# Opening, two attention starts and GpSimd's pieces rearranged in a two-layer transformer kernel

## The chip, the core and the metric

The kernel runs on one core of a Trainium2 chip. TensorE (PE) does the matrix products, VectorE (DVE), ScalarE (ACT) and GpSimd (POOL) the rest, and SyncE (SP) issues most of the DMA transfers. The metric is the device time of one execution in microseconds; less is better.

## What is computed

Two transformer layers in succession on 512 tokens of width 1024, in float32. The first has 16 meta tokens ahead of the sequence, and begins like this:

```python
xn = rms_norm(h, norm1_g)
p = xn @ w_in
(u_pool, q, c_lat, q_idx, k_idx, w_idx, cb, cc, cu, g_raw) = split_columns(p)
c_lat = rms_norm(c_lat, kv_norm_g)
attn = dsa_attention(q, q_idx, w_idx, c_lat, k_idx)   # scores by index heads choose 128 keys
h = h + (sigmoid gates over pooled, attention and convolution branches) @ w_o
h = h + (silu(gate) * up) @ w_down
```

The second layer has a feed-forward part, a mixer with two attentions (forgetting attention on 8 heads, stick-breaking attention on 8 heads), a second feed-forward part and a gated embedding.

## The kernel before

Everything lies transposed, features on the 128 partitions and tokens along the free dimension. The work is cut into 173 chunks of weights. A chunk has eight k-steps of 128 rows and 256 columns of weights (2048 columns per partition), and makes two output tiles, t = 0 and t = 1.

Each float32 operand is split into a high part (rounded to the matmul's type) and a low part (the rest), and each product is made of three matmuls: high by high, high by low, low by high (`passes`, L677 to L679). For the weights of a chunk this is a pipeline over four engines: SP loads `raw`, ScalarE copies the high part to `whi` (`high`, L1150, counted by `w_hi`), GpSimd subtracts to get the low part `wlo` (`low`, L561, in four pieces, counted by `w_lo`), and TensorE runs the chunk. There are two buffers, by the parity of the chunk: ScalarE begins with a chunk's high part when TensorE has ended the chunk two before. The input is split the same way, row by row of 128 features: `xh` on ScalarE (`gained`, L1155), `xl` on VectorE (`split`, L1602).

The order of the work on each engine is written out by hand, and semaphores join the engines; there is no planner.

The opening: chunk 0 (C_LAT) holds the latents. Its second tile is made by `index_tile`, which needs the index weights in a stacked tile, `stk`: the high part in columns 0 to 39, the low part in 64 to 103. ScalarE writes the high part behind the eighth row, GpSimd the low part (L580, `stk_lo`). Chunk 1 (C_QI) holds the index queries, chunks 2 to 5 (C_Q and on) the queries. Within chunk 1 come the norm sums (`norm_sums`, L746), for which VectorE adds up squares in `ssum`; then ScalarE takes a square root and VectorE a reciprocal (L1631), and the latents are scaled with it. VectorE splits `qst`, the stacked index queries, at L1767, and the scores of the index heads run between the k-steps of chunk 3 and on.

The first attention runs between the k-steps of four chunks, C_GB to C_GB + 3, by a list of slots:

```python
DSA_STEPS = {6 + n * 54 // (QB * HEADS + QB - 1): n for n in range(QB * HEADS + QB)}
```

In step n TensorE makes the logits of unit n + 2, transposes the probabilities of unit n and multiplies earlier ones with the values. VectorE copies a 16 x 16 corner out of PSUM (`dsa_edge`, L1934) and into its place (`dsa_edge_in`, L1943); TensorE waits for both.

The second layer's attentions run between the k-steps of chunks C_SQ and on, and before them stand eight head norms (`head_root` on ScalarE, `head_normed` on VectorE) and the values of chunk C_FV1 (`values_high` on ScalarE, `values_low` on VectorE, which frees the PSUM tile).

Of the kernel before, what the change touches and what calls it, by code (L numbers as in the profile page):

```python
# [82 lines left out]
DSA_STEPS = {6 + n * 54 // (QB * HEADS + QB - 1): n for n in range(QB * HEADS + QB)}  # L83

# [35 lines left out]
def build(nc, I, out):  # L120
    with ExitStack() as ctx:
# [265 lines left out]
        def _(sp):  # L387
# [46 lines left out]
            sp.dma_start(raw[:, 0, DK * P:DK * (P + KW)], I["w_lat"][:, DK * P:DK * (P + KW)]).then_inc(kw_in, 16)  # L434
# [106 lines left out]
        def _(pool):  # L541
# [37 lines left out]
            pool.wait_ge(stk_hi, 1)  # L579
            pool.tensor_tensor(stk[:, :, 64:64 + KW], raw[:, 0, DK * P:DK * (P + KW)].rearrange("p (k n) -> p k n", k=DK),  # L580
                               stk[:, :, 0:KW].bitcast(F32), ALU.subtract).then_inc(stk_lo, 1)
# [3 lines left out]
            run(C_Q, C_D[0], 2)  # L585
# [88 lines left out]
        def _(pe):  # L674
# [10 lines left out]
            def index_tile(b):  # L685

                pe.wait_ge(stk_lo, 1)
                for k in range(DK):
                    for z in range(2):
                        cs = slice(HALF * z, HALF * z + HALF)  # L690
                        if k:
                            pe.matmul(ps[0:KW, b + z, 0:HALF], stk[:, k - 1, 0:KW], xl[:, k - 1, cs], start=False, stop=False)
                        if k == DK - 1:
                            pe.matmul(ps[0:KW, b + z, 0:HALF], stk[:, k, 0:KW], xl[:, k, cs], start=False, stop=False)
                        mm = pe.matmul(ps[:, b + z, 0:HALF], stk[:, k, :], xh[:, k, cs], start=k == 0, stop=k == DK - 1)
                mm.then_inc(tile_done, 1)

            def chunk(c, hi, lo, per=0, i=None, X=None, full=(False, False), widths=(P, P), between=None, steps=None, ready=None):


                s, w = c % 2, sum(widths) if c != C_LAT else P
                if c not in (C_LAT, C_QI):
                    pe.wait_ge(w_lo, lin(c + 1, per, i))
                for t in range(2):
                    if C_GB < c < C_WB or C_SQ <= c < C_MX:
                        pe.wait_ge(acc_free, 2 * (c - 1) + t + 1)
                    elif c >= 2:
                        pe.wait_ge(acc_free, lin(2 * (c - 2) + t + 1, 2 * per, i))
                    b, m, o0 = bank(c, t), widths[t], sum(widths[:t])
                    if c == C_LAT and t == 1:  # L710
                        index_tile(b)
                        continue
                    for k in range(DK):
                        if X is not None:
                            x_ready(X, k, t)
                        if c in (C_LAT, C_QI) and t == 0 and k % 2 == 0:
                            if k < 6:
                                pe.wait_ge(lat_lo if c == C_LAT else qi_part_lo, k // 2 + 1)
# [85 lines left out]
            chunk(C_LAT, xh, xl, X=0, full=(True, True), widths=(P, KW))  # L804
            chunk(C_QI, xh, xl, steps=lambda t, k: norm_sums(0, C_QI) if (t, k) == (0, 5) else None)
# [333 lines left out]
        def _(act):  # L1139

            act.dma_start(vec[:, 0:V_ROWS], I["vec"]).then_inc(vec_in, 16)
            act.preload_act_table_set("sqrt_and_others")
# [33 lines left out]
            def root(S):  # L1176
                act.wait_ge(ss_done, S + 1)
                if S == 0:
                    act.activation(rt[:, 0:HALF], ps[:, 5, 0:HALF], ACT.Sqrt, bias=eps[:], scale=1.0 / D)
                    act.activation(rt[:, HALF:TM], ps[:, 7, 0:HALF], ACT.Sqrt, bias=eps[:], scale=1.0 / D).then_inc(rt_done, 1)  # L1180
# [45 lines left out]
            for n in range(DK):  # L1226
# [5 lines left out]
                if n == 0:  # L1232
# [3 lines left out]
            act.wait_ge(kw_in, 16)  # L1236
            act.wait_ge(stk_zero, 1)
            act.activation(stk[:, :, 0:KW], raw[:, 0, DK * P:DK * (P + KW)].rearrange("p (k n) -> p k n", k=DK),
                           ACT.Copy).then_inc(stk_hi, 1)
# [11 lines left out]
            high(C_LAT + 2)  # L1251
            act.wait_ge(ones_done, 1)
# [17 lines left out]
            act.activation(rt[:, 0:HALF], ps[:, 5, 0:HALF], ACT.Sqrt, bias=eps[:], scale=1.0 / D_LAT)  # L1270
            act.activation(rt[:, HALF:TM], ps[:, 7, 0:HALF], ACT.Sqrt, bias=eps[:], scale=1.0 / D_LAT).then_inc(crt_done, 1)
# [53 lines left out]
            with act.Fori(0, 2) as i:  # L1325
                for q in range(2):
# [5 lines left out]
                    high(c + 4, 6, i)  # L1332
# [26 lines left out]

            query_high(1)  # L1360
# [7 lines left out]
            dsa_unit(0)  # L1368
            dsa_unit(1)
            for slot in range(4 * 2 * DK):  # L1370
                n = DSA_STEPS.get(slot)
                if n is not None:
# [6 lines left out]
                    if n % QB == 1 and (n + 7) // QB < HEADS:  # L1379
                        query_high((n + 7) // QB)  # L1380
                    if n + 2 < QB * HEADS:
                        dsa_unit(n + 2)
                if slot % (2 * DK) == 2 * DK - 1:
                    high(C_GB + slot // (2 * DK) + 2)
# [100 lines left out]
            stack_high(F, 1, qF, kF, qt1, kt1)  # L1485
            head_root(6)
            head_root(7)
            for t in range(2):
                values_high(C_FV1, t, vF, 0)
# [102 lines left out]
        def _(dve):  # L1592
# [35 lines left out]
            def root(S):  # L1628
                lo = 0 if S == 0 else META
                dve.wait_ge(rt_done, S + 1)  # L1630
                dve.reciprocal(rs[:, lo:TM], rt[:, lo:TM]).then_inc(rs_done, 1)  # L1631
# [94 lines left out]
            dve.memset(eps[:], EPS)  # L1726
            dve.memset(stk[:].bitcast(F32), 0.0).then_inc(stk_zero, 1)
            dve.memset(ones[:].bitcast(F32), 1.0).then_inc(ones_done, 1)
# [5 lines left out]
            for n in range(DK):  # L1734
                split(0, n, V_N1, lo=0)
            dve.wait_ge(w_lo, C_LAT + 1)
# [12 lines left out]
            root(0)  # L1749
# [72 lines left out]
            dve.wait_ge(crt_done, 1)  # L1822
            link(dve.reciprocal(rc[:], rt[:]))
# [125 lines left out]

            for j in range(1, QB + 1):  # L1950
                link(dve.memset(pT[:, j, seen_from(j):P * j], 0.0))
            for n in range(2):
                dsa_unit(n)
                normalise(A, n, pr[:, n % 2, 0:META + P * (n % QB + 1)])
            query_low(1)
            for slot in range(4 * 2 * DK):
# [7 lines left out]
                if n % QB == QB - 1 and n >= QB:  # L1964
# [106 lines left out]
            head_normed(5)  # L2071
            head_normed(6)
            head_normed(7)
            for t in range(2):
                values_low(C_FV1, t, vF, 0, t + 3)
# [147 lines left out]
```

## Time and profile before

| | |
|---|---|
| median of 3 runs | 2006.44 us (2006.27 to 2006.93) |
| the profiled execution | 2006.25 us, span 2004.4 us |
| PE busy | 1989.6 us, 99% |
| POOL busy | 1007.8 us, 50% |
| DVE busy | 887.9 us, 44% |
| ACT busy | 730.2 us, 36% |
| the chain that ended last | 96% PE |

The span runs from the first to the last instruction of the profile, and the execution's time lies 1.85 us above it. PE's busy time counts the modelled ends of pipelined matmuls, so the distance from one start to the next tells more than the length of one. The column in brackets of a timeline is the idle time of the engine ahead of an instruction, and whose work ended it.

### The profile page before, as it was taken

To read this page: it belongs to the slowest core of one execution; us is meant where nothing else is said; L and a number is where in the kernel's file an instruction comes from. 1 tells how busy PE (TensorE), PEld (TensorE's weight loads), DVE (VectorE), ACT (ScalarE), POOL (GpSimd) and SP (SyncE) were. 2 spreads that over 40 slices of the span, in tenths; PEclk is the share of its full clock that TensorE was granted. 3 is DMA by queue.
4 is the path that set the end of the run, shared out by engine and by line. 5 is a ranking of instruction groups with operands and counts; after the bars stand their busy time and mean duration, and the time that the engine had idled before them with its cause. 6 is when DMAs were issued, how large, how long until landed. Compare 5 with 4: busy or idle time off the path is not lost.

```text
span 2004.4 us, 26695 instructions
## 1 busy us (share of the span) xinstructions
PE 1989.6 (99%) x9495; PEld 1667.9 (83%) x9495; DVE 887.9 (44%) x1468; ACT 730.2 (36%) x1017; POOL 1007.8 (50%) x780
## 2 busy tenths in 40 slices
PE   8999999999999999999999999999999999999999
PEld 7898887788888888888888888889888888888887
DVE  6687756634433222153333214677645533332124
ACT  6413224434323223232222225667643422222232
POOL 5344542245555554455555446665555555555443
PEclk9999999999999999999999999999999999999999
DMA  5223232123333322333332332332222333332232
GB/s 175 90 85 104 86 105 64 43 76 92 105 92 96 105 92 82 100 104 98 90 105 79 100 111 89 93 101 81 82 87 84 105 102 86 105 90 93 96 109 85
DMA packets 253787, 188.81 MB, mean 94 GB/s; under 512 B 6609, under 2 KB 249681, under 8 KB 253681
## 3 DMA queue, kind: packets, MB, share of 16 engines
q1 hardware_dynamic: 253024, 187.53, 31.4%
q8 instruction: 44, 0.72, 0.2%
q10 hardware_dynamic: 688, 0.31, 0.1%
q14 instruction: 31, 0.25, 0.0%
HBM read 180.93 MB, written 2.10 MB: 91 GB/s over the span
## 4 chain that ended last, share of the span: by engine, by line
PE 96%; DVE 1%; ACT 1%; issue 1%; DMA 0%; SPq 0%; DVEq 0%; ACTq 0%
PE ps L677 30%; PE ps L678 30%; PE ps L679 29%; PE ps L933 1%; PE ps L1085 1%; PE ps L1005 1%; PE ps L1006 1%; PE ps L1007 1%; PE ps L1073 1%; PE ps L1072 0%; PE ps L927 0%; DMA raw<-in_w_in 0%; DVE ssum L1748 0%; PE ps L1055 0%; PE ps L826 0%
## 5 line engine op out<-in xcount | busy, mean ns | idle before, releaser
L561 POOL TENSOR_TENSOR wlo<-raw,whi 128x512 fp32r<-128x512 f32 (+1 forms) x624 | 856.9, 1405 | 867.7 <-ACT whi L1150 850.3
L677 PE MATMUL ps<-xh,whi 128*128 128x512 f32 (+1 forms) x1888 | 722.2, 383 | 7.2 <-DVE xl L1602 5.8
L679 PE MATMUL ps<-xh,wlo 128*128 128x512 f32 (+1 forms) x1888 | 714.5, 378 | 0.0
L678 PE MATMUL ps<-xl,whi 128*128 128x512 f32 (+1 forms) x1888 | 714.4, 378 | 0.0
L1150 ACT ACTIVATE whi<-raw 128x2048 fp32r<-128x2048 f32 x154 | 289.6, 1881 | 775.1 <-PE ps L679 775.0
L677 PEld LDWEIGHTS ps<-xh,whi 128*128 128x128 f32 x1888 | 355.8, 188 | 72.2 <-DVE xl L1602 5.8
L679 PEld LDWEIGHTS ps<-xh,wlo 128*128 128x128 f32 x1888 | 355.6, 188 | 66.5
L678 PEld LDWEIGHTS ps<-xl,whi 128*128 128x128 f32 x1888 | 356.3, 189 | 61.8 <-issue 0.7
L1662 DVE TENSOR_TENSOR tmp<-ps,rs 128x512 f32<-128x512 f32 x148 | 101.9, 691 | 314.5 <-PE ps L679 297.0
L677 PE MATMUL ps<-fh,whi 128*128 128x512 f32 x528 | 205.4, 389 | 0.0
L678 PE MATMUL ps<-fl,whi 128*128 128x512 f32 x528 | 205.4, 389 | 0.0
L679 PE MATMUL ps<-fh,wlo 128*128 128x512 f32 x528 | 205.4, 389 | 0.0
L1602 DVE SCALAR_TENSOR_TENSOR hT<-ps,hT 128x512 f32 x40 | 27.6, 690 | 270.8 <-PE ps L679 269.9
L1687 DVE TENSOR_TENSOR tmp<-tmp 128x512 f32<-128x512 f32 x66 | 90.3, 1369 | 111.8 <-ACT tmp L1192 111.6
L679 PEld LDWEIGHTS ps<-fh,wlo 128*128 128x128 f32 x528 | 99.1, 188 | 20.7
L677 PEld LDWEIGHTS ps<-fh,whi 128*128 128x128 f32 x528 | 99.1, 188 | 20.5
L678 PEld LDWEIGHTS ps<-fl,whi 128*128 128x128 f32 x528 | 99.1, 188 | 20.5
L628 POOL TENSOR_TENSOR wlo<-raw,whi 128x384 fp32r<-128x384 f32 (+1 forms) x84 | 75.7, 933 | 38.2 <-ACT whi L1497 37.1
L1155 ACT ACTIVATE xh<-hT,vec (+1 forms) x48 | 34.7, 727 | 127.2 <-DVE hT L1602 125.2
L1194 ACT ACTIVATE fh<-tmp 128x512 f32 x66 | 41.8, 633 | 101.4 <-DVE tmp L1687 101.4
L1690 DVE TENSOR_TENSOR fl<-tmp,fh 128x512 f32 x66 | 50.9, 772 | 61.2 <-ACT fh L1194 61.2
L1602 DVE SCALAR_TENSOR_TENSOR xl<-hT,vec,xh (+1 forms) x48 | 45.6, 955 | 57.9 <-ACT xh L1155 57.9
(324 smaller groups left out, 2215.3 us busy)
## 6 DMA issues: line engine op xcount, KB each, us to landing
raw<-in_w_in SPq DMA_DIRECT2D x87, 512.0 KB, 4.6
raw<-in_w_gate_up SPq DMA_DIRECT2D x44, 512.0 KB, 4.6
raw<-in_ffn_w_gate SPq DMA_DIRECT2D x44, 512.0 KB, 4.0
raw<-in_ffn_w_up SPq DMA_DIRECT2D x44, 512.0 KB, 5.2
raw<-in_ffn_w_down SPq DMA_DIRECT2D x32, 512.0 KB, 4.1
raw<-in_w_down SPq DMA_DIRECT2D x16, 512.0 KB, 4.0
raw<-in_ffn_w_down SPq DMA_DIRECT2D x16, 384.0 KB, 3.7
raw<-in_w_b SPq DMA_DIRECT2D x8, 512.0 KB, 4.0
```

Of the source, the lines that this page charges most:

```text
L561: ins = pool.tensor_tensor(wlo[:, c % 2, cs], raw[:, c % 2, cs], whi[:, c % 2, cs].bitcast(F32), ALU.subtract)
L628: ins = pool.tensor_tensor(wlo[:, c % 2, cs], raw[:, c % 2, cs], whi[:, c % 2, cs].bitcast(F32), ALU.subtract)
L677: pe.matmul(o, w_of(whi), xhi, start=first, stop=False)
L678: pe.matmul(o, w_of(whi), xlo, start=False, stop=False)
L679: return pe.matmul(o, w_of(wlo), xhi, start=False, stop=last)
L1150: act.activation(whi[:, c % 2, 0:n], raw[:, c % 2, 0:n], ACT.Copy).then_inc(w_hi, 1)
L1155: act.activation(one(xh, nn)[:, lo:TM], one(hT, nn)[:, lo:TM], ACT.Copy, scale=col(vec, lin(gain + n, per, i))).then_inc(xh_done, 1)
L1194: act.activation(one(fh, lin(n, per, i)), tmp[:, 3, :], ACT.Copy).then_inc(h_hi, 1)
L1602: return dve.scalar_tensor_tensor(o, a, s, b, op0, op1)
L1662: dve.tensor_tensor(o, ps[0:o.shape[0], bank(c, t), :], rsx[0:o.shape[0]], ALU.mult).then_inc(acc_free, 1)
L1687: dve.tensor_tensor(tmp[:, 3, :], tmp[:, 1, :], tmp[:, 2, :], ALU.mult).then_inc(h_done, 1)
L1690: dve.tensor_tensor(one(fl, nn), tmp[:, 3, :], one(fh, nn).bitcast(F32), ALU.subtract).then_inc(h_split, 1)
```

## The change

- Opening: ten matmuls on `ones` run first on TensorE, into a bank not yet in use. The latents and the index weights' tile, one after the other before, are now interleaved by rows: three rows of latents, then the wait for `stk_lo`, then rows of both in turn. The index weights are loaded, copied (ScalarE) and reduced (now on VectorE) behind the third row instead of behind the eighth.
- Chunk 2's weights go through ScalarE and GpSimd in four quarters, for which TensorE waits one by one, as chunk 1's did. The norm sums move from (t, k) = (0, 5) to (1, 2).
- The root of the first norm and that of the latents' norm become Ln and Exp on ScalarE, without VectorE's reciprocal.
- GpSimd's `low` works in eight pieces instead of four, in every chunk that goes through it.
- First attention: ScalarE's weight copies of three chunks go as quarters into slots without a step; its last weight copy before the attention is taken out of the loop, which is unrolled. On VectorE the first two units stand ahead of the clearing of `pT`, and `dsa_edge(n)` ahead of `dsa_edge_in(n - 1)`.
- Second layer: the copies of the first value tile of C_FV1 move ahead of the last two head roots and norms.

```diff
+FREE_SLOTS = [slot for slot in range(4 * 2 * DK) if slot not in DSA_STEPS]
...
                 sp.dma_start(hT[:, n, :], I["h0"][P * n:P * n + P, :]).then_inc(x_in[n], 16)
-            sp.dma_start(raw[:, 0, DK * P:DK * (P + KW)], I["w_lat"][:, DK * P:DK * (P + KW)]).then_inc(kw_in, 16)
+                if n == 2:
+                    sp.dma_start(raw[:, 0, DK * P:DK * (P + KW)], I["w_lat"][:, DK * P:DK * (P + KW)]).then_inc(kw_in, 16)
...
             sp.wait_ge(stk_lo, 1)
+            sp.wait_ge(w_lo, C_LAT + 1)
...
             def low(c, per=0, i=None):
-                n = n_cols(c) // 4
+                n = n_cols(c) // 8
                 pool.wait_ge(w_hi, lin(c + 1, per, i))
-                for part in range(4):
+                for part in range(8):
...
+            for z in range(4):
+                if z < 3:
+                    pool.wait_ge(qi_part_hi, 4 + z)
+                else:
+                    pool.wait_ge(w_hi, C_Q + 1)
+                cs = slice(CH // 4 * z, CH // 4 * z + CH // 4)
+                pool.tensor_tensor(wlo[:, 0, cs], raw[:, 0, cs], whi[:, 0, cs].bitcast(F32),
+                                   ALU.subtract).then_inc(qi_part_lo if z < 3 else w_lo, 1)
...
+            def index_row(k):
...
+                    if k:
+                        pe.matmul(ps[0:KW, b + z, 0:HALF], stk[:, k - 1, 0:KW], xl[:, k - 1, cs], start=False, stop=False)
+                    if k == DK - 1:
+                        pe.matmul(ps[0:KW, b + z, 0:HALF], stk[:, k, 0:KW], xl[:, k, cs], start=False, stop=False)
+                    mm = pe.matmul(ps[:, b + z, 0:HALF], stk[:, k, :], xh[:, k, cs], start=k == 0, stop=k == DK - 1)
...
+            def opening():
+
+                pe.wait_ge(ones_done, 1)
+                for n in range(10):
+                    pe.matmul(ps[:, 7, :].rearrange("p (a t) -> p a t", a=4), ones[:],
+                              ones[:].unsqueeze(1).to_broadcast([P, 4, P]), start=True, stop=True)
+                for k in range(3):
+                    latent_row(k)
+                    latent_low(k)
                 pe.wait_ge(stk_lo, 1)
...
+                index_row(0)
+                index_row(1)
+                for k in range(3, DK):
+                    latent_row(k)
+                    index_row(k - 1)
+                    latent_low(k)
+                index_row(DK - 1)
...
+            opening()
+            chunk(C_QI, xh, xl, steps=lambda t, k: norm_sums(0, C_QI) if (t, k) == (1, 2) else None)
...
+                    act.activation(rt[:, 0:HALF], ps[:, 5, 0:HALF], ACT.Ln, bias=eps[:], scale=1.0 / D)
+                    act.activation(rt[:, HALF:TM], ps[:, 7, 0:HALF], ACT.Ln, bias=eps[:], scale=1.0 / D).then_inc(rt_done, 1)
+                    act.wait_ge(rt_done, 1)
+                    act.activation(rs[:], rt[:], ACT.Exp, scale=-0.5).then_inc(rs_done, 1)
...
+                if j and z < 4:
+                    high_quarter(C_GB + j + 1, z)
...
+                if n == 2:
+                    dve.wait_ge(stk_hi, 1)
+                    dve.tensor_tensor(stk[:, :, 64:64 + KW], raw[:, 0, DK * P:DK * (P + KW)].rearrange("p (k n) -> p k n", k=DK),
+                                      stk[:, :, 0:KW].bitcast(F32), ALU.subtract).then_inc(stk_lo, 1)
...
+                if n < QB * HEADS:
+                    dsa_edge(n)
                 if 1 <= n <= QB * HEADS:
                     dsa_edge_in(n - 1)
-                if n < QB * HEADS:
-                    dsa_edge(n)
...
+            values_low(C_FV1, 0, vF, 0, 3)
             head_normed(6)
             head_normed(7)
-            for t in range(2):
-                values_low(C_FV1, t, vF, 0, t + 3)
+            values_low(C_FV1, 1, vF, 0, 4)
```

`latent_row(k)` makes the high by high and low by high matmuls of the latents' row k (four of 264 columns), `latent_low(k)` the two with `xl`.

## Rows read from the trace of the kernel before

**Rows 1.** The page, busy time by engine.

```profile
PE 1989.6 (99%) x9495; PEld 1667.9 (83%) x9495; DVE 887.9 (44%) x1468; ACT 730.2 (36%) x1017; POOL 1007.8 (50%) x780
```

**Rows 2.** TensorE's waits: releaser, us in total, times, longest.

```profile
PE ps L677 <- DVE xl L1602: 5.8, 1, 5.8
PE ps L677 <- DVE vF L1602: 1.4, 1, 1.4
PE ps L933 <- DVE edge L1934: 1.4, 4, 0.7
PE ps L927 <- DVE edge L1934: 0.9, 2, 0.7
PE ps L746 <- DVE ssum L1748: 0.7, 1, 0.7
```

**Rows 3.** Timeline of TensorE, opening: start, length (us), line, operands, count.

```profile
11.37 0.28 PE L677 MATMUL ps<-xh,whi 128*128 128x264 f32 x1
...
18.17 0.39 PE L677 MATMUL ps<-xh,whi 128*128 128x512 f32 x1
...
23.13 1.16 PE L746 MATMUL ps<-ssum,ones 128*128 128x264 f32 x4 [0.69 <-DVE ssum L1748]
...
30.94 0.39 PE L677 MATMUL ps<-xh,whi 128*128 128x512 f32 x1
...
36.38 1.05 PE L812 MATMUL ps<-sq,ones 128*128 128x264 f32 x4
...
43.29 0.39 PE L677 MATMUL ps<-xh,whi 128*128 128x512 f32 x1
```

**Rows 4.** Timeline of GpSimd, opening and a feed-forward stage.

```profile
3.76 0.73 POOL L577 TENSOR_TENSOR wlo<-raw,whi 128x256 fp32r<-128x256 f32 x1 [0.51 <-ACT whi L1230]
...
33.90 7.01 POOL L561 TENSOR_TENSOR wlo<-raw,whi 128x512 fp32r<-128x512 f32 x4 [3.84 <-ACT whi L1150]
...
45.55 5.03 POOL L561 TENSOR_TENSOR wlo<-raw,whi 128x512 fp32r<-128x512 f32 x4 [4.63 <-ACT whi L1150]
...
559.66 5.94 POOL L561 TENSOR_TENSOR wlo<-raw,whi 128x512 fp32r<-128x512 f32 x4 [4.94 <-ACT whi L1150]
```

**Rows 5.** Timeline of ScalarE, opening.

```profile
7.00 1.41 ACT L1155 ACTIVATE xh<-hT,vec 128x528 fp32r<-128x528 f32 x2 [0.38 <-DMA hT<-in_h]
...
12.17 0.45 ACT L1238 ACTIVATE stk<-raw 128x320 fp32r<-128x320 f32 x1
...
31.93 1.90 ACT L1150 ACTIVATE whi<-raw 128x2048 fp32r<-128x2048 f32 x1
```

**Rows 6.** Timeline of VectorE, opening.

```profile
7.76 1.45 DVE L1602 SCALAR_TENSOR_TENSOR xl<-hT,vec,xh 128x528 fp32r<-128x528 f32 x2 [0.65 <-ACT xh L1155]
...
25.27 3.45 DVE L1631 RECIPROCAL rs<-rt 128x528 f32<-128x528 f32 x1 [2.20 <-ACT rt L1180]
...
35.34 7.90 DVE L1767 TENSOR_TENSOR qst<-qiT,qih 32x1024 fp32r<-32x1024 f32 x4 [1.20 <-ACT qih L1263]
```

**Rows 7.** Timeline of SyncE, opening: the index weights' transfer.

```profile
6.42 0.43 SPq L434 DMA_DIRECT2D raw<-in_w_lat  x1
```

**Rows 8.** VectorE's line L1767: ns min/median/max, first and last start.

```profile
L1767 DVE TENSOR_TENSOR qst<-qiT,qih x4: 1219/2192/2204, 35.3 to 42.0; 32x1024 fp32r<-32x1024 f32 x4
```

**Rows 9.** Timeline of VectorE, first attention.

```profile
359.33 1.21 DVE L1943 COPY pT<-edge 16x16 f32<-16x16 f32 x1
```

**Rows 10.** Timeline of GpSimd, first attention.

```profile
359.23 5.67 POOL L561 TENSOR_TENSOR wlo<-raw,whi 128x512 fp32r<-128x512 f32 x4 [20.74 <-ACT whi L1150]
```

**Rows 11.** Timeline of ScalarE, end of the first attention.

```profile
395.18 0.60 ACT L1349 ACTIVATE pT<-ps 128x512 f32<-128x512 f32 x1
...
404.63 1.92 ACT L1150 ACTIVATE whi<-raw 128x2048 fp32r<-128x2048 f32 x1 [1.64 <-PE ps L679]
```

**Rows 12.** Timeline of VectorE and ScalarE, before the second attention.

```profile
1276.69 3.38 DVE L1602 SCALAR_TENSOR_TENSOR kF<-qs,vec,rtq 128x512 f32<-128x512 f32 x2
...
1283.26 1.55 ACT L1433 ACTIVATE vF<-ps,rtok 128x256 fp32r<-128x256 f32 x4
```

More of the change, by code:

```diff
@@ L683, in x_ready @@
                     pe.wait_ge(x_split, DK * X + k + 1)
-            def index_tile(b):
-                pe.wait_ge(stk_lo, 1)
[L688 to L696, printed above, removed]
+            def index_row(k):
+                b = bank(C_LAT, 1)
+                for z in range(2):
+                    cs = slice(HALF * z, HALF * z + HALF)
+                    if k:
[3 more added lines that the diff above has]
+                    mm = pe.matmul(ps[:, b + z, 0:HALF], stk[:, k, :], xh[:, k, cs], start=k == 0, stop=k == DK - 1)
+                if k == DK - 1:
+                    mm.then_inc(tile_done, 1)
@@ new lines, in latent_row @@
+            def latent_row(k):
+                b, w = bank(C_LAT, 0), slice(P * k, P * k + P)
+                halves = [(ps[:, b + z, 0:HALF], slice(HALF * z, HALF * z + HALF)) for z in range(2)]
+                pe.wait_ge(xh_done, k + 1)
+                for o, cs in halves:
+                    pe.matmul(o, whi[:, 0, w], xh[:, k, cs], start=k == 0, stop=False)
+                if k % 2 == 0:
+                    if k < 6:
+                        pe.wait_ge(lat_lo, k // 2 + 1)
+                    else:
+                        pe.wait_ge(w_lo, C_LAT + 1)
+                for o, cs in halves:
+                    pe.matmul(o, wlo[:, 0, w], xh[:, k, cs], start=False, stop=False)
@@ new lines, in latent_low @@
+            def latent_low(k):
+                w = slice(P * k, P * k + P)
+                pe.wait_ge(x_split, k + 1)
+                for z in range(2):
+                    mm = pe.matmul(ps[:, bank(C_LAT, 0) + z, 0:HALF], whi[:, 0, w], xl[:, k, HALF * z:HALF * z + HALF],
+                                   start=False, stop=k == DK - 1)
+                if k == DK - 1:
+                    mm.then_inc(tile_done, 1)
+            def opening():
[6 more added lines that the diff above has]
+                    latent_low(k)
+                pe.wait_ge(stk_lo, 1)
+                index_row(0)
[5 more added lines that the diff above has]
+                index_row(DK - 1)
@@ L698, in chunk @@
             def chunk(c, hi, lo, per=0, i=None, X=None, full=(False, False), widths=(P, P), between=None, steps=None, ready=None):
-                s, w = c % 2, sum(widths) if c != C_LAT else P
-                if c not in (C_LAT, C_QI):
+                s, w = c % 2, sum(widths)
+                if c not in (C_QI, C_Q):
                     pe.wait_ge(w_lo, lin(c + 1, per, i))
@@ L715, in chunk @@
                             x_ready(X, k, t)
-                        if c in (C_LAT, C_QI) and t == 0 and k % 2 == 0:
+                        if c in (C_QI, C_Q) and t == 0 and k % 2 == 0:
                             if k < 6:
-                                pe.wait_ge(lat_lo if c == C_LAT else qi_part_lo, k // 2 + 1)
+                                pe.wait_ge(qi_part_lo, 3 * (c - C_QI) + k // 2 + 1)
                             else:
@@ L1250, in _ @@
                 act.activation((sq, rt)[n % 2][:], hT[:, n, :], ACT.Square).then_inc(sq_done, 1)
-            high(C_LAT + 2)
-            act.wait_ge(ones_done, 1)
+            for z in range(4):
+                if z == 0:
+                    act.wait_ge(raw_in[0], raw_level(C_Q, 0, None))
+                    act.wait_ge(tile_done, 2 * C_LAT + 2)
+                cs = slice(CH // 4 * z, CH // 4 * z + CH // 4)
+                act.activation(whi[:, 0, cs], raw[:, 0, cs], ACT.Copy).then_inc(qi_part_hi if z < 3 else w_hi, 1)
             root(0)
@@ L1324, in _ @@
             act.preload_act_table_set("sigmoid_and_others")
-            with act.Fori(0, 2) as i:
+            for i in range(2):
                 for q in range(2):
@@ L1368, in _ @@
             dsa_unit(0)
+            high_quarter(C_GB + 1, 0)
             dsa_unit(1)
+            high_quarter(C_GB + 1, 1)
             for slot in range(4 * 2 * DK):
                 n = DSA_STEPS.get(slot)
+                j = slot // (2 * DK)
+                z = FREE_SLOTS.index(slot) - len([f for f in FREE_SLOTS if f < 2 * DK * j]) if slot in FREE_SLOTS else 4
+                if j and z < 4:
+                    high_quarter(C_GB + j + 1, z)
                 if n is not None:
@@ L1724, in project @@
                 split_sums(S)
-            dve.memset(eps[:], EPS)
+            dve.memset(ones[:].bitcast(F32), 1.0).then_inc(ones_done, 1)
+            dve.memset(eps[:], EPS).then_inc(ones_done, 1)
             dve.memset(stk[:].bitcast(F32), 0.0).then_inc(stk_zero, 1)
-            dve.memset(ones[:].bitcast(F32), 1.0).then_inc(ones_done, 1)
             dve.memset(ctok[:, QB, :], 0.0).then_inc(ctok_zero, 1)
@@ L1748, in _ @@
                 dve.tensor_tensor(ssum[:], ssum[:], (sq, rt)[n % 2][:], ALU.add).then_inc(ssum_done, 1)
-            root(0)
+            dve.wait_ge(rs_done, 1)
             scaled_full(cl[:], C_LAT, 0)
@@ L1948, in query_low @@
                 dve.tensor_tensor(ath[:, h, P:T], qT[:, h, P:T], qh[:, h, P:T].bitcast(F32), ALU.subtract).then_inc(q_split, 1)
+            dsa_unit(0)
+            dsa_unit(1)
+            for n in range(2):
+                normalise(A, n, pr[:, n % 2, 0:META + P * (n % QB + 1)])
             for j in range(1, QB + 1):
                 link(dve.memset(pT[:, j, seen_from(j):P * j], 0.0))
-            for n in range(2):
-                dsa_unit(n)
-                normalise(A, n, pr[:, n % 2, 0:META + P * (n % QB + 1)])
             query_low(1)
```

50 lines of the change are left out of this document (23 added, 27 removed).

## The prediction

> **What bounds the kernel now.** I read the page first: TensorE is busy for 99% of the span [rows 1], so a change can win only what TensorE waits for, or what it runs at the low clock. The view of waits, TensorE alone, gives nearly the whole of that as a list [rows 2]: 5.8 us before the first matmul, 0.7 us for `ssum`, 1.4 us for an evacuation of `vF`, and 1.4 + 0.9 us for `edge`, six times, in the first attention. Then I read the stretch of each wait on the timeline, engine by engine.
>
> The opening [rows 3]: the first matmul starts at 5.8 us. The 24 matmuls of 264 columns up to 11.37 us take 0.232 us each; the next 56 (24 of the latents, 32 of the index weights) end at 18.17 us, 0.121 us each. That is the step from the 1.2 to the 2.4 GHz level, 5.6 us after TensorE's first work. From 18.17 us on it is chunk 1 (C_QI), with a hole of 0.69 us for `ssum` before the norm sums at 23.13 us; chunk 2 (C_Q) starts at 30.94, chunk 3 at 43.29 us. A matmul of 512 columns takes (36.38 - 30.94)/24 = 0.227 us.
>
> In the rest TensorE is fed in time. In the feed-forward stages GpSimd's low weights take 5.94 us, and it idles 4.94 us in each period of 10.88 us [rows 4]. So the three places of waits, and new waits that the edits make, decide.
>
> **The opening, part by part.** Ten matmuls of 512 columns on `ones` are added ahead. At 0.232 us per 264 columns they take 4.5 us; with VectorE's memset of `ones` put first I let them start at 1.1 to 1.3 us (an estimate), so they end about where the first row came anyway. If the clock rises 5.6 us after the first work again, that is at 6.7 to 6.9 us. The bounds are at once and, if they do nothing, 11.37 us as now.
>
> TensorE then takes three rows of latents (18 matmuls) and waits for `stk_lo`, the join. ScalarE's third row ends at 7.0 + 0.7 = 7.7 us and the moved copy of the index weights takes 0.45 us [rows 5]: 8.15 us. VectorE's third split ends at 7.76 + 0.73 = 8.5 us, and the low part, moved there from GpSimd, has 320 of the split's 528 columns, so 0.45 us [rows 6]: about 9.05 us with the handovers. What is left is 62 matmuls (6 + 5 x 10 + 6), 7.5 us at 0.121: chunk 1 can begin at 16.6 us instead of 18.17.
>
> The moved transfer of the index weights occupies SP for 0.43 us [rows 7] and now stands ahead of five rows. Those rows also pass the copy on ScalarE and the low part on VectorE, so each comes at most 0.9 us later. Today the last row is split by 13.56 us (latents end at 18.17 - 32 x 0.121 = 14.29 us, less the six matmuls of that row); with 0.9 us added that is 14.5, and TensorE asks for it only at 16.6 - 8 x 0.121 = 15.6 us. So this costs nothing, with 1.1 us of cover. The index weights were already ahead of chunk 1's on that queue, so chunk 1's come no later.
>
> Chunk 1: the norm sums move from its 6th to its 11th k-step. TensorE is there at 16.6 + 33 x 0.227 = 24.1 us, past the 23.13 us at which `ssum` came: the 0.7 us wait goes. The sums took 1.0 us (30 matmuls of 0.227 lie between 24.14 and 30.94). After: 25.1 us, 15 matmuls more, chunk 2 at 28.5 us instead of 30.94: **-2.4 us**.
>
> The root: VectorE's reciprocal of 3.45 us [rows 6] becomes an Exp on ScalarE of the same 528 columns, no more than the 0.7 us of the copies there [rows 5]. The chain behind the sums gets 2.75 us shorter. Chunk 2 waits for the evacuated latents: their scaling, one operation of 0.7 us behind the reciprocal, ended at 25.27 + 3.45 + 0.7 = 29.4 us, 5.3 us after TensorE resumed behind the sums at 24.14; it will be 2.55 us, and chunk 2 asks 3.4 us after. The second reciprocal (`rc`) goes likewise; no row of waits names it, so I count nothing. The unrolled loop on ScalarE also counts nothing: ScalarE is not waited for there.
>
> Chunk 3 is where I expect a new wait. Now GpSimd starts its low weights at 33.90 us, 9.76 us after TensorE resumed behind the sums (24.14). After, that is 9.76 - 2.75 = 7.0 us behind the resumption at 25.1. TensorE needs them 3.4 + (43.29 - 30.94) = 15.75 us behind it: 8.75 us for GpSimd's work. Undisturbed, four pieces take 5.03 us [rows 4]. One piece of 256 columns took 0.73 us [rows 4], eight at most 5.84; pieces overlap a little, and I take 5.5. But four operations of VectorE on `qst` fall into that stretch, and rows show the two engines taking turns: such an operation lasts 1.22 us alone and 2.19 us beside GpSimd [rows 8], and GpSimd's four pieces took 7.01 instead of 5.03 us [rows 4], 0.98 us for each of two operations let in between. Eight pieces leave room for all four: 5.5 + 3.9 = 9.4 us, **0.65 us too late**. Bounds: none let in, 5.0 us and no wait; 5.84 + 4 x 1.22 = 10.7 us, 2.0 us late. I take 0.65, nearest to the 7.01 us row.
>
> The Trainium skill (SBUF — State Buffer, section "SBUF: two separate sides") says that the port pair of VectorE and GpSimd "is an exclusive lock, not a bandwidth split", held for the whole instruction. It speaks against eight pieces here, since every border between pieces lets the other engine in: by that rule chunk 2's gain of 2.4 us shrinks to 1.75 as above; by a split of bandwidth the number of pieces would not matter, the work would end in time, and the sum would be 0.65 us better. The 2.19 against 1.22 us [rows 8] agree with the lock.
>
> The opening in sum: -2.4 + 0.65 = **-1.75 us**.
>
> **The first attention.** Six waits, two lines [rows 2]: the copy that TensorE waits for stood behind `dsa_edge_in`, a 16 x 16 copy that took up to 1.21 us at 359.33 us [rows 9] while GpSimd's low weights ran from 359.23 us [rows 10]. Exchanged, the awaited copy no longer stands behind it; the one moved back is asked for a step later. ScalarE's weight copies, one of 1.9 us each [rows 5], are cut into quarters in slots without an attention step, so one step is delayed by a quarter at most. The start: the query copy and the first two exponentials no longer stand behind a whole weight copy, and GpSimd's pieces come after the first steps. Of 2.3 us [rows 2] I take **-1.9 us**; bounds 0 and 2.3. The quarters of the last chunk there finish at slot 57 of 64; GpSimd needs 5.5 to 5.84 us after it. ScalarE's copy for slot 53 lies at 395.18 us and the next chunk starts at 404.6 us [rows 11]: two quarters of about 0.6 us and 5.84 us end near 402.5 us, 2 us of cover.
>
> **The second attention's start.** Chunk C_SQ waited 1.4 us for the evacuation of C_FV1's first tile. Its copies on ScalarE (two of four in 1.55 us [rows 12], 0.75 us) move ahead of two head roots, VectorE's part ahead of two norms. The evacuation then is early, but the last root comes 0.75 us later, and the first scores wait for it. Against this, two norms that took 3.38 us beside GpSimd [rows 12] (0.7 each undisturbed) get through sooner with pieces half as long. I take **-1.0 us**; bounds 0 and 1.4.
>
> **Eight pieces elsewhere** cost GpSimd 0.5 to 0.8 us per chunk, plus perhaps one more turn of VectorE. The cover is the 4.94 us idle [rows 4]; without it each of some 150 chunks would pay. Counted nothing.
>
> **Sum.** -1.75 - 1.9 - 1.0 = -4.65 us. The profiled execution took 2006.25 us (span 2004.4), so 2001.6; the median of the runs lies 0.19 above it: **2001.8 us**.
>
> **The rivals.**
> Chunk 3 is not kept waiting: GpSimd gets ahead before VectorE's four operations. For it speaks that two pieces were through before the first of them; against it the 2.19 us. 2001.1 us.
>
> The attentions give little: lows now at other times meet other steps, and the late root eats the second start. With 0.6 and 0.4 us in place of 1.9 and 1.0: 2003.7 us. For it speaks that each step there hangs on three engines; against it that the waits have named causes.
>
> The change's warm-up does nothing: clock at 11.37 us. From 9.05 us ten matmuls slow, 52 fast: chunk 1 at 17.7 us, chunk 2 at 29.6, -1.35 + 0.65 = -0.7 us, 2002.9 us in sum. Against it: at the low rate the rows keep TensorE busy without holes.
>
> The other side: the half rate holds on. Each us of it behind 9.05 us costs half a us; the gain is gone if it lasts to about 18.3 us, and the kernel is slower by 0.2% from about 26 us. Through the opening and chunk 1: 62 x 0.232 = 14.4 us, then 48 x 0.453 us and sums twice as long: chunk 2 at 47.6 us, 2006.44 + 16.7 + 0.65 - 2.9 = 2020.9 us. For it speaks only that 18 matmuls followed by a wait for the join may leave holes.
>
> **Numbers.** Forecast 0.40 (own range 2000.9 to 2002.4), no wait at chunk 3 0.17, little from the attentions 0.27, no warm-up effect 0.08, half rate kept 0.05; 0.03 for no net change. 0.2% is 4.0 us, about what can be told from no change: the border is 2002.4 us. Faster 0.40 + 0.17 = 0.57; same 0.27 + 0.08 + 0.03 = 0.38; slower 0.05. The range goes from everything gained (2.4 + 2.3 + 1.4 = 6.1, 2000.3, half a us lower for the bounds of the join) to just past the weak attentions: 1999.8 to 2004.2 us.
>
> **What would show it.** Right: matmuls of 264 columns at 0.121 us before 8 us; chunk 1 near 16.6, no wait for `ssum`, chunk 2 near 28.5 us; a wait of about 0.65 us for GpSimd's weights at chunk 3 near 41 us; no `edge` rows; the `vF` wait gone and a shorter one before the scores. Wrong: the 0.232 us past 9 us; `stk_lo` later than 9.5 us; TensorE waiting for low weights in any later chunk.

## The result and the profile after

The changed kernel is slower: 2012.29 us median of 9 runs (2012.0 to 2012.86) against 2006.29 us of the kernel before, a ratio of 1.0031 (95% interval 1.0022 to 1.0039). The profiled execution has a span of 2010.2 us.

The page's busy time by engine; GpSimd's grew by 111 us [rows 1]:

```profile
PE 1998.3 (99%) x9505; PEld 1667.1 (83%) x9505; DVE 840.2 (42%) x1467; ACT 732.9 (36%) x1034; POOL 1119.2 (56%) x1399
```

TensorE's waits (releaser, us in total, times, longest):

```profile
PE ps L688 <- POOL wlo L566: 4.1, 11, 0.8
PE ps L738 <- DVE eps L1796: 1.1, 1, 1.1
PE ps L978 <- DVE pT L2015: 1.0, 1, 1.0
PE ps L1136 <- DVE pu L1984: 0.8, 1, 0.8
```

The old waits for `ssum`, `vF` and `edge` [rows 2] are gone, and the first one has shrunk from 5.8 to 1.1 us. In the place of `edge` stands one wait of 1.0 us for the other small copy, `pT`. New is the first row: `low` (L566, before L561) makes TensorE wait, and the chain that ended last lies on GpSimd for 23%.

The list of waits understates this. A wait shows only as idle time beyond the modelled end of the matmul ahead, and short ones don't show. So I set the start of each TensorE instruction against that of the same instruction before (after minus before, us):

| place | offset |
|---|---|
| chunk 2 starts | -3.05 |
| chunk 3 starts | -2.33 |
| end of the first attention | -4.59 |
| last chunk of the first projections starts | -2.96 |
| end of feed-forward 0 (down stage) | -0.05 |
| end of feed-forward 1 | +1.9 |
| through the second attention's start | +1.5 |
| end of the second projections | +4.3 |
| end | +5.75 |

The opening and the first attention gained 4.6 us, where 3.65 was forecast for these two. Behind them 10.3 us are lost, nearly all in steps of 0.25 to 1.1 us, each at the start of a chunk of a projection, merge or down stage or at the border of one. One of them, on GpSimd's timeline and then TensorE's:

```profile
764.60 5.60 POOL L566 TENSOR_TENSOR wlo<-raw,whi 128x256 fp32r<-128x256 f32 x8 [5.91 <-ACT whi L1201]
```

```profile
769.60 0.39 PE L690 MATMUL ps<-fh,wlo 128*128 128x512 f32 x1
770.25 0.50 PE L688 MATMUL ps<-fh,whi 128*128 128x512 f32 x1 [0.26 <-POOL wlo L566]
```

The low weights end at 764.60 + 5.60 = 770.20 us and the chunk starts at 770.25, where 769.60 + 0.227 = 769.83 was due: 0.42 us lost, of which the view of waits shows 0.26. The same place in the kernel before, on GpSimd's and TensorE's timelines:

```profile
767.07 5.03 POOL L561 TENSOR_TENSOR wlo<-raw,whi 128x512 fp32r<-128x512 f32 x4 [6.52 <-ACT whi L1150]
```

```profile
772.35 0.39 PE L677 MATMUL ps<-fh,whi 128*128 128x512 f32 x1
```

Four pieces ended at 772.10 us, 0.25 us ahead of need. GpSimd had sat idle for 6.52 us ahead of them, but waiting for ScalarE's copy of the weights, which stands behind the work on a residual row (`feed`) in this stage: that idle time was no cover. Eight pieces cost 5.60 - 5.03 = 0.57 us more, 0.14 for each piece added, and 0.25 us of it was covered.

In the second projections it is more. GpSimd's and TensorE's timelines of the kernel before:

```profile
1515.02 5.52 POOL L561 TENSOR_TENSOR wlo<-raw,whi 128x512 fp32r<-128x512 f32 x4 [8.64 <-ACT whi L1150]
```

```profile
1520.77 0.39 PE L677 MATMUL ps<-yfh,whi 128*128 128x512 f32 x1
```

and of the changed kernel:

```profile
1516.55 6.51 POOL L566 TENSOR_TENSOR wlo<-raw,whi 128x256 fp32r<-128x256 f32 x8 [8.06 <-ACT whi L1201]
```

```profile
1523.19 0.49 PE L688 MATMUL ps<-yfh,whi 128*128 128x512 f32 x1 [0.72 <-POOL wlo L566]
```

The cover was 1520.77 - 1520.54 = 0.23 us, and the work became 0.99 us longer: 0.57 for the pieces, and about 0.4 that fits one more operation of VectorE let in between (a reading of the lengths: GpSimd's eight pieces take 5.6, 6.05 or 6.5 us, in steps of 0.45). TensorE lost 0.9 us here.

### The profile page after: what moved, and what is told of

The parts are those of the page before. It is cut to its first block, busy times and chain, and to the rows that moved or that the text cites. A ratio compares the mean times of both kernels' runs of the same rounds, so it can differ in the third digit from the quotient of the medians.

```text
span 2010.2 us, 27311 instructions
## 1 busy us (share of the span) xinstructions
PE 1998.3 (99%) x9505; PEld 1667.1 (83%) x9505; DVE 840.2 (42%) x1467; ACT 732.9 (36%) x1034; POOL 1119.2 (56%) x1399
## 4 chain that ended last, share of the span: by engine, by line
PE 54%; POOL 23%; issue 22%; ACT 1%; DVE 0%; POOLq 0%; ACTq 0%
POOL wlo L566 22%; PE ps L688 16%; PE ps L689 16%; PE ps L690 16%; PE ps L1136 1%; PE ps L1056 1%; PE ps L1057 1%; PE ps L1058 1%; PE ps L1124 1%; PE ps L1123 0%; POOL wlo L591 0%; PE ps L1106 0%; PE ps L1094 0%; PE ps L738 0%; PE ps L1105 0%
## 5 line engine op out<-in xcount | busy, mean ns | idle before, releaser
L566 POOL TENSOR_TENSOR wlo<-raw,whi 128x256 fp32r<-128x256 f32 (+1 forms) x1240 | 964.2, 814 | 764.0 <-ACT whi L1201 676.1
L1201 ACT ACTIVATE whi<-raw 128x2048 fp32r<-128x2048 f32 (+1 forms) x149 | 280.1, 1880 | 805.8 <-PE ps L690 805.7
L688 PEld LDWEIGHTS ps<-xh,whi 128*128 128x128 f32 x1872 | 351.7, 188 | 68.0 <-POOL wlo L566 2.6
L690 PEld LDWEIGHTS ps<-xh,wlo 128*128 128x128 f32 x1872 | 351.4, 188 | 66.7
L689 PEld LDWEIGHTS ps<-xl,whi 128*128 128x128 f32 x1872 | 352.0, 188 | 61.7 <-issue 0.7
L1756 DVE TENSOR_TENSOR tmp<-tmp 128x512 f32<-128x512 f32 x66 | 54.4, 824 | 112.3 <-ACT tmp L1246 112.0
L1759 DVE TENSOR_TENSOR fl<-tmp,fh 128x512 f32 x66 | 59.4, 899 | 62.3 <-ACT fh L1248 62.3
```

Source lines behind the costliest of these rows:

```text
L688: pe.matmul(o, w_of(whi), xhi, start=first, stop=False)
L689: pe.matmul(o, w_of(whi), xlo, start=False, stop=False)
L690: return pe.matmul(o, w_of(wlo), xhi, start=False, stop=last)
L1201: act.activation(whi[:, c % 2, 0:n], raw[:, c % 2, 0:n], ACT.Copy).then_inc(w_hi, 1)
L1756: dve.tensor_tensor(tmp[:, 3, :], tmp[:, 1, :], tmp[:, 2, :], ALU.mult).then_inc(h_done, 1)
L1759: dve.tensor_tensor(one(fl, nn), tmp[:, 3, :], one(fh, nn).bitcast(F32), ALU.subtract).then_inc(h_split, 1)
```

## The experiments

Times are medians of 5 to 11 runs, taken in three groups; the kernel before, in each of them, took 2006.10, 2006.08 and 2006.35 us, so a difference between versions of different groups is good to about 0.3 us. "After" in a diff is the changed kernel.

**Four pieces again** (`e1_four`), everything else as changed:

```diff
-                n = n_cols(c) // 8
+                n = n_cols(c) // 4
...
-                for part in range(8):
+                for part in range(4):
```

> The changed kernel with GpSimd's low weights in four pieces again, everything else as changed. Theory (missed cover): the losses behind the first attention are 1.6 us in the first projections, 2.9 + 0.65 in feed-forward 0, 1.3 in feed-forward 1, 2.8 in the second projections, 1.3 in feed-forward 2, some 9.9 us in all (with the piece at the second attention's start), all of them TensorE's waits for the low weights, and chunk 3's 0.6 us; without them 2012.3 - 9.9 - 0.6 = 2001.8 us (2001.0 to 2002.8), and the row of TensorE's waits for the low weights is gone. Rival (the losses come from the rest of the change: the moved copies and the new order put every later chunk at another phase against VectorE's operations, and the pieces only show where the wait is booked): above 2008 us.

2004.08 us, ratio 0.999 (0.9981 to 0.9999): 8.2 us of the changed kernel's time were the pieces', and no wait for the low weights is left. The expected 2001.8 was missed by 2.3 us. The offsets show where: -1.66 at the start of the first attention and -1.83 at its end. With four pieces the attention gains next to nothing. VectorE's and GpSimd's timelines there:

```profile
316.62 0.15 DVE L2015 COPY pT<-edge 16x16 f32<-16x16 f32 x1
...
318.82 0.16 DVE L2006 COPY edge<-ps 16x16 f32<-16x16 f32 x1
318.91 0.91 DVE L2015 COPY pT<-edge 16x16 f32<-16x16 f32 x1
...
319.92 1.20 DVE L1984 TENSOR_SCALAR pr<-pr,rden 128x144 f32<-128x144 f32 x1
```

```profile
316.78 5.50 POOL L566 TENSOR_TENSOR wlo<-raw,whi 128x512 fp32r<-128x512 f32 x4 [13.65 <-ACT whi L1341]
```

A 16 x 16 copy of 0.15 us takes 0.91 us beside GpSimd's four pieces (316.78 to 322.28 us), and TensorE waits 1.4 us for it. In the changed kernel the same copy took 0.38 us, and the wait was 1.0 us. TensorE loses another 1.0 us at 350 to 353 us and 0.3 at 398 us, which the changed kernel doesn't.

**Eight pieces alone** (`e2_eight_only`): the kernel before, with the two edited lines of `low` and nothing else.

> The kernel before with GpSimd's low weights in eight pieces and nothing else. Theory (missed cover): the same tight chunks pay, so +9 to +10.5 us, 2015 to 2017 us, with a row of TensorE's waits for the low weights of 4 us or more. Rival (the rest of the change): within 2 us of the kernel before.

2016.02 us, ratio 1.005 (1.0037 to 1.0064): +9.9 us, with this row among TensorE's waits:

```profile
PE ps L677 <- POOL wlo L561: 3.8, 11, 0.8
```

So the loss doesn't come from the reordered work; the edit of two lines makes it by itself. In its attention TensorE's offset moved by only 0.3 us: eight pieces alone hardly help there.

**Eight pieces in the up stages alone** (`e5_eight_up`):

```diff
-            run(C_Q + 2, C_D[0], 2)
+            run(C_Q + 2, C_F[0], 2)
+            run(C_F[0], C_D[0], 2, 8)
...
-            run(C_F[1], C_D[1], 2)
+            run(C_F[1], C_D[1], 2, 8)
...
-            run(C_MX + 2, C_D[2], 2)
+            run(C_MX + 2, C_F[2], 2)
+            run(C_F[2], C_D[2], 2, 8)
```

The last argument of `run` is the number of pieces, four without it.

> The changed kernel with eight pieces only in the up stages of the three feed-forward parts (66 chunks, where the trace of before showed GpSimd idle for 4.94 us a period) and four everywhere else. Theory (cover): these chunks pay nothing, though each costs GpSimd 0.57 us more: within 0.6 us of the version with four pieces throughout. Rival (eight pieces cost TensorE or VectorE something wherever they run, by turns on memory): 66/150 of the losses, 4 us above the version with four pieces.

2005.65 us, 1.57 us above the version with four pieces: more than the 0.6 expected, less than the rival's 4. The offsets between these two profiles put 1.5 of 1.6 us behind the opening at four places, 0.35 at 490, 0.25 at 849, 0.6 at 873 and 0.3 at 1585 us, at the border of such a stage with a projection or a down stage or two chunks behind it. At these places the kernel before had 0.6 to 0.9 us of cover, and in the changed kernel GpSimd's work is 1.0 us longer there, not 0.57. In the rest of these stages nothing moves. There a chunk starts 2.75 us after its low weights end: 559.66 + 5.94 = 565.60 us [rows 4], and this row of the kernel before, TensorE's timeline:

```profile
568.35 0.39 PE L677 MATMUL ps<-xh,whi 128*128 128x512 f32 x1
```

**Eight pieces, ScalarE's copy earlier** (`e6_copy_first`): in the projections, the two merge stages and the down stages, in the same way in each:

```diff
+                        high(c + j + 2, 2, i)
                         act.wait_ge(acc_free, lin(2 * (c + j) + 2, 4, i))
                         feed(S, 2 * j + 1, gain, 4, i)
-                        high(c + j + 2, 2, i)
```

> The changed kernel, eight pieces throughout, but ScalarE's weight copy of the next chunk stands ahead of the second row's work (feed or merged) in the projections, the merge stages and the down stages, so that GpSimd can begin up to 2.7 us earlier in the projections and 1.2 us or more in the others. Theory (missed cover): the 9 us come back although GpSimd's work is as long as in the changed kernel: 2002 to 2005 us. Rival (eight pieces themselves disturb TensorE or VectorE): stays within 2 us of 2012.3. A third possibility, that the rows fed 1.9 us later are late for the next stage, would show as new waits for xh or ssum of up to 2 us a stage.

2006.19 us: 6.1 us come back with GpSimd's work as long as in the changed kernel (1138.0 us busy). The down stages keep steps of 0.35 us, and 2002 to 2005 was missed by a little. So it is cover, in the main; the next run shows that the earlier copy alone gains nothing.

**Four pieces, the copy earlier** (`e7_four_copy_first`): both edits together.

> The changed kernel with four pieces throughout, and ScalarE's weight copy ahead of the second row's work in the projection, merge and down stages. Theory (cover): with four pieces the low weights end ahead of TensorE's need there already, so an earlier copy wins nothing: 2004.1 us, within 0.6 us of the version with four pieces in the old order. Rival (the earlier copy gains by itself, and that is what made the eight-piece version with it faster): up to 6 us less, 1998 to 2003 us.

2011.34 us, 7.3 us slower than four pieces in the old order; neither theory had it. TensorE's waits name the place, the norm sums at the end of four stages (set against the version with four pieces in the old order, each costs 1.5 us; a fifth, near 855 us, costs 1.3):

```profile
PE ps L805 <- DVE ssl L1707: 5.0, 4, 1.3
```

VectorE's timeline of the first of them, four pieces:

```profile
492.79 1.77 DVE L1688 TENSOR_TENSOR ssum<-ssum,sq 128x512 f32<-128x512 f32 x1
494.60 1.40 DVE L1706 CAST ssh<-ssum 128x512 fp32r<-128x512 f32 x1
496.03 1.64 DVE L1707 TENSOR_TENSOR ssl<-ssum,ssh 128x512 fp32r<-128x512 f32 x1
```

and with eight pieces in the same order:

```profile
492.27 1.22 DVE L1688 TENSOR_TENSOR ssum<-ssum,sq 128x512 f32<-128x512 f32 x1
493.52 0.85 DVE L1706 CAST ssh<-ssum 128x512 fp32r<-128x512 f32 x1
494.40 1.11 DVE L1707 TENSOR_TENSOR ssl<-ssum,ssh 128x512 fp32r<-128x512 f32 x1
```

In the old order the same three took 0.69, 0.43 and 0.69 us, since GpSimd began only with the last of them. The earlier copy puts GpSimd's pieces beside VectorE's last operations of the stage, and each then gets 0.95 to 1.1 us longer beside pieces of 512 columns, 0.4 to 0.5 beside pieces of 256. So short pieces are worth something where VectorE's chain is awaited, and cost something where GpSimd's own end is.

**Eight pieces only in the first attention** (`e3_eight_in_attention`):

```diff
-            run(C_Q + 2, C_D[0], 2)
+            run(C_Q + 2, C_GB, 2)
+            low(C_GB)
+            for c in range(C_GB + 1, C_WB + 1):
+                low(c, pieces=8)
+            low(C_WB + 1)
+            run(C_WB + 2, C_D[0], 2)
```

> The changed kernel with eight pieces only in the four chunks whose low weights are made during the first attention (C_GB + 1 to C_WB) and four everywhere else. Theory (short pieces help exactly there): with four pieces throughout the first attention gained only 0.1 us (TensorE waited 1.4 + 0.6 us for VectorE's 16 x 16 copies, one of which took 0.91 us beside GpSimd's pieces), with eight it gained 2.3 us; so 2.0 us below the version with four pieces throughout, 2002.1 us (2001.3 to 2003.0). Rival (the attention's gain depends on where its steps fall, not on the pieces): within 0.6 us of 2004.1.

2001.65 us, ratio 0.9978 (0.9969 to 0.9987): the fastest version, 2.4 us below four pieces throughout and 10.6 below the changed kernel. The offset against the kernel before goes from -2.6 at chunk 3 to -4.95 behind the attention and ends at -4.66 us. The next four experiments start from it.

**Whole copies in the attention** (`e12_whole_copies`): that version with ScalarE's weight copies as before.

```diff
-                if j and z < 4:
-                    high_quarter(C_GB + j + 1, z)
...
+                if slot % (2 * DK) == 2 * DK - 1:
+                    high(C_GB + slot // (2 * DK) + 2)
```

> The version with eight pieces only in the first attention, but with ScalarE's weight copies of its chunks whole and at the ends of the chunks, as in the kernel before. Theory (short pieces and quarters are both needed: the kernel before with eight pieces gained 0.3 us over the attention, the changed kernel 2.3 us): 1.5 to 2.3 us slower than with quarters, 2003.2 to 2004.0 us, and TensorE's waits for the 16 x 16 copies back. Rival (the pieces alone do it): within 0.6 us of 2001.65.

2003.0 us, 1.35 us slower (1.1 when each is set against the kernel before in its own group), a little under the expected 1.5: about half of the attention's gain is the quarters', and it needs the short pieces as well. The new order at the attention's start was not taken out alone.

**The old order of the two small copies** (`e10_old_edge`):

```diff
-                if n < QB * HEADS:
-                    dsa_edge(n)
                 if 1 <= n <= QB * HEADS:
                     dsa_edge_in(n - 1)
+                if n < QB * HEADS:
+                    dsa_edge(n)
```

> The version with eight pieces only in the first attention, with the copy into pT ahead of the copy out of PSUM on VectorE again, as in the kernel before. Theory of the prediction (the exchange takes the awaited copy from behind a 16 x 16 copy of up to 1.2 us): up to 1.9 us slower and edge rows among TensorE's waits. Rival (either order leaves one of the two copies awaited, and the pieces decide): within 0.6 us.

2001.63 us: no difference. TensorE's 1.0 us wait is the same, with `edge` as its releaser in place of `pT`.

**The values behind the roots again** (`e9_values_last`): `values_high` and `values_low` of C_FV1 both behind `head_root(7)` and `head_normed(7)`.

> The version with eight pieces only in the first attention, with the copies of the first value tile of C_FV1 behind the last two head roots and norms again, as in the kernel before. Theory of the prediction: its move wins 1.0 us at the second attention's start, so 1.0 us slower. Rival (what it wins at chunk C_SQ is lost again at the first scores, as the offsets of the version with four pieces show: 1.1 us won there, 1.5 us lost within the next 3 us): within 0.5 us, and TensorE's wait of about 1.4 us for vF is back.

2001.66 us: no difference. The wait for `vF` is back,

```profile
PE ps L693 <- DVE vF L1677: 1.4, 1, 1.4
```

with 1.5 us of offset at chunk C_SQ, of which 1.2 us are gone again 2.5 us later, at the first transposed weights of the attention.

**No warm-up** (`e4b_no_warm`): the ten matmuls on `ones` left out; nothing of the result uses them.

> The version with eight pieces only in the first attention, without the ten matmuls on ones ahead of the opening. Theory (the clock rises a fixed time behind TensorE's first work): the first row comes at 5 to 6 us and the matmuls of 264 columns take 0.232 us until 10 to 11.4 us instead of 0.121 from 7 us on; that delays the opening by about 1.1 to 2 us, so 1 to 2 us more than with them. Rival (the opening waits for its rows and for the join anyway): within 0.5 us.

2002.13 us, 0.5 us more, within the rival's bound and not clear of the scatter (2001.55 to 2003.34, against 2001.28 to 2002.2). TensorE's timeline without them:

```profile
5.31 0.78 PE L720 MATMUL ps<-xh,whi 128*128 128x264 f32 x2 [5.31 <-ACT xh L1208]
...
9.30 0.61 PE L727 MATMUL ps<-xh,wlo 128*128 128x264 f32 x2
9.74 0.41 PE L734 MATMUL ps<-xl,whi 128*128 128x264 f32 x2
9.98 0.40 PE L710 MATMUL ps<-xh,stk 128*128 128x264 f32 x2
```

The spacing halves from 0.22 to 0.12 us at 9.7 us, 4.4 us behind the first work; in the profile with them it halves at 5.7 us, and chunk 1 starts 1.0 us earlier (16.53 against 17.53). Most of this isn't the warm-up's. ScalarE's second row, which waits for its transfer, came at 6.58 us in this profile and at 5.72 in the other; with the warm-up and a row at 6.53 (`e6_copy_first`) or 6.68 us (`e1_four`) chunk 1 starts at 17.34 or 17.41, only 0.1 to 0.2 us before 17.53. Nor does the clock rise a fixed time behind the first work, as the theory has it: with the first of the ten matmuls at 1.08 us the spacing halves at 4.6 us in `e1_four` and at 7.2 us in the changed kernel.

**The opening alone** (`e11_opening_alone`): four pieces throughout, and the edits of both attentions undone.

> The new opening alone: four pieces throughout, both attentions in the order of the kernel before, ScalarE's weight copies of the first attention whole. Theory: the opening is worth 1.7 to 2.6 us in the four profiles with four-piece or mixed kernels, and with four pieces neither attention gains; so 2006.1 - 2.0 = 2004.1 us (2003.4 to 2004.6), the time of the version with four pieces throughout. Rival (the order of the attentions is worth something with four pieces too): 2005 us or more.

2004.73 us, ratio 0.9992 (0.9983 to 1.0001): 1.6 us for the opening, between the theory's range and the rival's. That is 0.65 us above four pieces with the new attentions (0.4 when each is set against its own group), so those bring little without short pieces. In the profile the opening has gained 2.9 us at chunk 3, and 0.4 of it is lost again in the attention in its old order.

**Sixteen pieces** (`e2b_sixteen_only`): the kernel before with `// 16` and `range(16)`.

> The kernel before with sixteen pieces and nothing else; twelve pieces more by 0.14 us each are 1.7 us a chunk (2.3 us and more where VectorE is let in oftener). Theory (cover): the chunks of the projection, merge and down stages have 0.2 to 0.9 us of cover, and some 30 of them pay what is beyond it; eight pieces cost 10 us by using up the cover and 0.3 us on average beyond it, so the second doubling costs 1.14 us or more on each of some 30 to 36 chunks: 2016.0 + 34 to 55 = 2050 to 2071 us. The up stages, with 4.9 us of cover, still pay nothing. Rival (a cost per piece wherever it runs): 10 us per four pieces, 2006.1 + 30 = 2036 us.

2058.16 us, +51.8 us, and 41.9 for the second doubling where the first cost 9.9. Some 6.4 us of it are a lower clock behind four of the waits (last section). Without them too the loss is more than proportional to the pieces (30 for twelve), as is to be expected of a cover that is used up first. In the up stage of feed-forward 0 TensorE's offset stands still at 10.1 us from 492 us to the first down chunk.

## Why the prediction was wrong

The step that failed is **Eight pieces elsewhere**: "The cover is the 4.94 us idle [rows 4] ... Counted nothing." The cost per chunk was right (0.5 to 0.8 us and perhaps a turn of VectorE forecast; 0.57 measured in most chunks, 1.0 in many of the tight ones). The cover was taken from one stage and from the wrong gap. GpSimd's idle time ahead of its work was time in which it had no input; what covers a longer work is the time from its end to TensorE's need, 2.75 us in the up stage and 0.25 us at 772 us. Read in this way, the kernel before has 0.2 to 0.9 us in the first projections and merge stage (chunks that start at 426 to 492 us) and 0.2 to 1.0 us in the second ones (1520 to 1586 us), so the loss could have been seen beforehand. It is also what the forecast itself named as its sign of being wrong, a wait for low weights in a later chunk. Its size by the runs: 1.6 us for the up stages with their borders; for the other chunks, 2012.29 - 2004.08 + 2.4 (the attention's gain given back by four pieces) - 1.6 = 9.0 us, of which the 0.7 at chunk 3 was forecast.

**The opening**: -1.75 us forecast with the wait at chunk 3. The 1.6 us measured alone are with four pieces, where no such wait comes and the forecast's terms give 2.4; so the near agreement is in part luck. In the profile after it is better in its steps: chunk 1 at 16.04 us (16.6 forecast), chunk 2 at 27.89 (28.5), no wait for `ssum`. The new wait at chunk 3 cost 0.73 us (0.65 forecast), and its mechanism was right: GpSimd's work took 9.54 us (9.4 forecast) beside VectorE's four operations on `qst`. GpSimd's timeline, then TensorE's:

```profile
31.37 9.54 POOL L566 TENSOR_TENSOR wlo<-raw,whi 128x256 fp32r<-128x256 f32 x8 [1.92 <-ACT whi L1201]
```

```profile
40.97 0.50 PE L688 MATMUL ps<-xh,whi 128*128 128x512 f32 x1 [0.56 <-POOL wlo L566]
```

How much the opening gains depends on when its rows land. In the ten profiles with the new opening and the warm-up ScalarE starts the second row at 4.85 to 6.68 us, and chunk 1 begins 10.7 to 11.2 us behind it, from 16.04 to 17.41 us; the changed kernel's profile is the earliest of them, so its good steps are in part luck. In the three profiles with the old opening the same distance is 12.6 to 13.1 us. At a like landing the opening thus gains about 2 us at chunk 1, where 1.6 was forecast. The warm-up is worth about 0.5 us by the timed runs, and less by the rows, rather than the 1.1 between forecast and rival.

**The first attention**: -1.9 us forecast, -2.3 in the profile after. The size was right by luck, the reason for the most part wrong: the forecast put first the exchanged copies, whose worth is 0.0 us. It also named the quarters, which are about half of the gain, but not the short pieces, without which next to nothing is left; together they are worth -2.4 us.

**The second attention's start**: -1.0 us forecast, 0.0 measured. The rival "the late root eats the second start" holds for this half: the awaited thing at chunk C_SQ comes sooner, and the first scores' comes later.

**The port**: the forecast weighed the Trainium skill (SBUF — State Buffer, section "SBUF: two separate sides"), an exclusive lock held for a whole instruction. The rows above agree with it: what a VectorE operation loses beside GpSimd, 0.95 to 1.1 us against 0.4 to 0.5, halves with the piece, and stays under the length of one (5.03/4 = 1.26 and 5.60/8 = 0.70 us). It wasn't used where it speaks for eight pieces, in the first attention and the ends of the stages.

**The sum**: the version with eight pieces in the first attention alone has the forecast's time, 2001.65 against 2001.8 us, but with -1.6, -2.4 and 0.0 in place of -1.75, -1.9 and -1.0, and with four pieces where eight were not free. That the times agree is luck. The measured terms sum to -4.0 us where the version gained 4.4; the missing 0.4 fits what the opening alone loses again in the old attention.

Open: no run separates, in the tight chunks, VectorE's turns from the pieces' own 0.57 us; the split above is read from lengths alone. Nor do the runs show what sets when the opening's rows land.

## What to carry to other kernels

Idle time of an engine ahead of its work is cover only if its input is there. Otherwise the cover is the distance from its end to its consumer's need, and it has to be read once in every kind of stage, not in the roomiest. Where GpSimd and VectorE meet, the length of GpSimd's instructions sets VectorE's delay and their number GpSimd's own end: choose the pieces by stage, short where VectorE's chain is awaited, long where GpSimd's end is. A wait that is removed by exchanging two operations is only won if the second consumer has slack.

## What was not expected of the hardware

TensorE can lose its clock in a short wait. In the run with sixteen pieces waits of 2.0 to 2.1 us for the low weights, three in the down stage of feed-forward 0 and one at the chunk behind it, were followed by some 3.4 us at a granted clock of 0.50, the lower of the two levels (1.2 GHz), with matmuls 0.43 us apart instead of 0.23. The view of windows (stretch, us, TensorE's busy time, granted clock, DMA share, GB/s), around two of these waits, which ended at 773.85 and 807.77 us:

```profile
768.00:771.00 3.00, 3.00 (x15) 1.00 0.00 0
...
776.00:778.00 2.00, 2.00 (x7) 0.59 0.82 286
778.00:781.00 3.00, 3.00 (x14) 1.00 0.00 0
...
809.00:811.50 2.50, 2.50 (x7) 0.50 0.91 308
```

All four such waits show it, and each cost another 1.6 us, not much less than the wait itself. Behind a wait of 2.54 us, which ended at 1133.67 us, the clock stayed at 1.00, so the length of the wait alone doesn't decide; what else does, these runs don't show.
